# Seven of the 24 modulation chunks of a two-layer diffusion trunk are weighed on the vector engine instead of the tensor engine

## The reference, cut to what matters

```python
mod = jax.nn.silu(cvec) @ w_mod[l] + b_mod[l]            # (1024,) @ (1024, 6144), one row for each of the 2 blocks
sh1, sc1, g1, sh2, sc2, g2 = jnp.split(mod[:, None, :], 6, axis=-1)
h = rms_norm(x, norm_mix[l]) * (1.0 + sc1) + sh1
x = x + g1 * mixer(h)       # l = 0: differential attention and gated DeltaNet; l = 1: gated MLP with a spatial product
h = rms_norm(x, norm_ffn[l]) * (1.0 + sc2) + sh2
x = x + g2 * hier_moe(h)    # 32 experts in 4 groups, the best 2 of one group for each token
```

## Time and profile before

| what | value |
|---|---|
| time, median of 3 runs (lowest to highest) | 803.41 us (802.33 to 806.38) |
| the profiled execution: its own time / its span | 802.09 / 800.3 us |
| PE busy, share of the span | 738.1 us, 92% |
| PE weight loads busy | 490.7 us, 61% |
| DVE busy / ACT busy / POOL busy | 307.1 us (38%) / 163.0 us (20%) / 18.1 us (2%) |
| DMA traffic | 291.49 MB, mean 364 GB/s |
| mean granted PE clock | 0.976 |

### The profile page before, as it was taken

How to read it: one execution, slowest core, us unless ns; L and a number is a source line. 1 busy time by engine, 2 the same in 40 slices (tenths; PEclk the granted TensorE clock), 3 DMA queues, 4 the chain that set the end, 5 groups by cost and what they waited for, 6 DMA issues and landing times.

```text
span 800.3 us, 15774 instructions
## 1 busy us (share of the span) xinstructions
PE 738.1 (92%) x6831; PEld 490.7 (61%) x6831; DVE 307.1 (38%) x680; ACT 163.0 (20%) x319; POOL 18.1 (2%) x29
## 2 busy tenths in 40 slices
PE   3999999998999999999967799999999999995887
PEld 2788467677789745655544244689965655553435
DVE  1144668572512633433440232224353433443024
ACT  3113231233212411111110033031141111111013
POOL 0000001011210000000000000001000000000000
PEclk9999999999999999999998899999999999998798
DMA  9999979496899899999999999999689999999992
GB/s 341 386 372 382 344 267 350 160 327 215 249 373 405 335 422 421 408 421 419 422 420 416 402 386 386 386 406 389 215 314 423 417 399 420 421 421 421 415 399 97
DMA packets 90648, 291.49 MB, mean 364 GB/s; under 512 B 11769, under 2 KB 14927, under 8 KB 73167
## 3 DMA queue, kind: packets, MB, share of 16 engines
q1 hardware_dynamic: 79728, 284.32, 91.0%
q10 hardware_dynamic: 10847, 6.12, 2.7%
HBM read 288.32 MB, written 2.10 MB: 363 GB/s over the span
## 4 chain that ended last, share of the span: by engine, by line
PE 74%; SPq 13%; DMA 7%; ACT 2%; DVE 2%; issue 2%; ACTq 0%; DVEq 0%
PE psum L1346 7%; PE psum L928 7%; PE psum L1430 7%; PE psum L1445 7%; SPq L768 6%; PE psum L1420 6%; PE psum L1480 5%; PE psum L1007 5%; PE psum L881 5%; PE psum L1621 3%; PE psum L1639 3%; PE psum L1491 3%; SPq L786 3%; PE psum L1072 2%; DMA wrt<-in_w_router_expert 2%; DMA ring<-in_w_exp_up 2%
## 5 line engine op out<-in xcount | busy, mean ns | idle before, releaser
L1430 PE MATMUL psum<-ring,hT 128*32 128x512 f32 (+1 forms) x304 | 74.5, 612 | 12.4 <-DMA scratch<-in_w_exp_up 12.4
L1430 PE MATMUL psum<-scratch,hT 128*32 128x512 f32 (+1 forms) x368 | 74.5, 624 | 11.8 <-DMA ring<-in_w_exp_up 11.8
L1420 PE MATMUL psum<-scratch 128*128 128x128 f32 x640 | 75.5, 276 | 0.0
L1420 PEld LDWEIGHTS psum<-scratch 128*128 128x128 f32 x640 | 73.2, 192 | 1.7 <-issue 1.7
L928 PE MATMUL psum<-hT,ring 128*128 128x256 f32 x256 | 57.8, 382 | 1.1 <-DVE hT L2186 0.6
L928 PEld LDWEIGHTS psum<-hT,ring 128*128 128x128 f32 x256 | 47.8, 190 | 9.6 <-DVE hT L2186 2.0
L1491 PEld LDWEIGHTS psum<-const,scratch 128*128 128x128 bf16 x432 | 40.5, 97 | 18.2 <-issue 12.4
L1491 PE MATMUL psum<-const,scratch 128*128 128x256 bf16 x432 | 50.4, 272 | 0.2 <-DVE scratch L2638 0.2
L2003 ACT ACTIVATE scratch<-psum 128x256 f32<-128x256 f32 x20 | 7.7, 384 | 198.1 <-PE psum L1430 124.5
L2631 DVE TENSOR_SCALAR hT<-psum,const 128x512 f32<-128x512 f32 x20 | 15.0, 751 | 85.7 <-PE psum L1480 84.2
L1430 PEld LDWEIGHTS psum<-ring,hT 128*32 128x32 f32 (+1 forms) x304 | 19.7, 117 | 43.3 <-issue 43.3
(11 more groups left out here) (354 smaller groups left out, 991.8 us busy)
## 6 DMA issues: line engine op xcount, KB each, us to landing
ring<-in_w_mod SPq DMA_DIRECT2D x40, 1024.0 KB, 11.7
scratch<-in_w_exp_down SPq DMA_DIRECT2D x32, 1024.0 KB, 17.0
ring<-in_w_exp_down SPq DMA_DIRECT2D x24, 1024.0 KB, 18.1
scratch<-in_w_exp_gate SPq DMA_DIRECT2D x22, 1024.0 KB, 17.5
scratch<-in_w_exp_up SPq DMA_DIRECT2D x22, 1024.0 KB, 19.5
ring<-in_w_exp_gate SPq DMA_DIRECT2D x18, 1024.0 KB, 17.4
ring<-in_w_exp_up SPq DMA_DIRECT2D x18, 1024.0 KB, 20.1
scratch<-in_w_exp_gate SPq DMA_DIRECT2D x24, 512.0 KB, 9.1
```

The lines of the kernel that those rows point to most:

```text
L1420: last = mm(bank[b][:, k * P:(k + 1) * P], hrow[:, t, half * 4 + k, :], Pm[:, t, :], start=(t == 0), stop=(t == 1))
L1430: last = mm(bank[0][i * m:(i + 1) * m, :], xg[:, k, i * m:(i + 1) * m], w[e][:, k, :, :], start=(k == 0), stop=(k == KT - 1))
```

## The change

The matrix product of a chunk is a sum over the 8 rows `k` and over the 128 partitions. For the seven chunks in `SUMMED` the sum over `k` moves to DVE: `weigh_rows` goes over the 8 rows and the 2 token blocks with one instruction of 128 x 512 each, the first two a product with a scalar, the other 14 a fused multiply-add, and leaves the two sums in rows 0 and 1 of the chunk's own slot. PE then only adds over the partitions, with stationary operands [1 0] and [0 1]: 8 products in place of 32. Each `weigh_rows` waits until the whole chunk has landed, and PE waits for the new semaphore `v_acc`. Four further things move: PE uses (0,7) and (0,9) where (0,6) and (0,8) stood, and (0,6) and (0,8) after them; (1,5) follows `in1` 3; in the middle SP loads (1,10) ahead of `in1` 0 and (1,11) ahead of `in1` 1; the turning of group `M_B` is later on all three engines. `v_abx` and `t_u` are folded into other semaphores.

```diff
+SUMMED = [(0, 6), (0, 8), (0, 10), (0, 11), (1, 5), (1, 10), (1, 11)]
...
-        put_mods(0, 6, 7)
+        put_mods(0, 7, 6)
         put("in0", 0)
-        put_mods(0, 8, 9)
+        put_mods(0, 9, 8)
...
+        middle = [index[s] for s in (("mod", 1, 4), ("in1", 2), ("mod", 1, 5), ("in1", 3), ("mod", 1, 10), ("in1", 0), ("mod", 1, 11),
+                                     ("in1", 1), ("out1", 0), ("out1", 1))]
...
+        chosen = [const[:, C_J8 - 1:C_J8 + 1], const[:, C_I32:C_I32 + 2]]
...
@@ mod_chunk, PE
-                if g > M_HI and nth == 0:
+                if g > M_HI:
                     pe.wait_ge(S.v_mod, g)
+                if (l, j) in SUMMED:
+                    pe.wait_ge(S.v_acc, 2 * KT * (SUMMED.index((l, j)) + 1))
+                    for t in range(NB):
+                        for m in range(4):
+                            last = mm(bank[mbank[g]][32 * m:32 * m + NB, at:at + P], chosen[t], w[:, 1 - t, m * P:(m + 1) * P],
+                                      start=(t == 0), stop=(t == NB - 1))
+                    used(last)
+                    return
...
@@ PE, layer 0
             last.then_inc(S.t_ab, 1)
-            mod_chunk(0, 6)
+            mod_chunk(0, 7)
             pe.wait_ge(S.a_sqc, 2)
...
             length_sums()
-            mod_chunk(0, 7)
             length_rows()
+            mod_chunk(0, 6)
...
-            mod_chunk(0, 8)
+            mod_chunk(0, 9)
             pe.wait_ge(S.a_qkv, 1)
...
-            mod_chunk(0, 9)
+            mod_chunk(0, 8)
...
@@ PE, the middle
             for j in range(2):
-                if j == 1:
-                    mod_chunk(1, 5)
                 s = chunk_full(pe, ("in1", 2 + j))
...
-            mod_turn(M_B)
+            mod_chunk(1, 5)
...
@@ DVE
+            def weigh_rows(l, j, k0=0, k1=KT):
+
+                w = slot_kn(chunk_full(dve, ("mod", l, j)))
+                done = 2 * KT * SUMMED.index((l, j))
+                early = part(E0 + 8704, (512,)) if (l, j) in ((0, 6), (0, 8)) else const[:, C_LEV:C_LEV + 512]
+                for k in range(k0, k1):
+                    for t in range(NB):
+                        out = early if t == 0 and k < 2 else w[:, 1 - t, :]
+                        if k == 0:
+                            if t == 1:
+                                dve.wait_ge(S.v_acc, done + 1)
+                            ins = V.tensor_scalar(out, w[:, k, :], condT[:, t, k:k + 1], None, ALU.mult)
+                        else:
+                            dve.wait_ge(S.v_acc, done + (4 if k == 2 else 2 * k - 1 + t))
+                            ins = V.scalar_tensor_tensor(out, w[:, k, :], condT[:, t, k:k + 1], early if t == 0 and k == 2 else out, ALU.mult, ALU.add)
+                        ins.then_inc(S.v_acc, 1)
...
             conv_rows(2)
+            weigh_rows(0, 6)
             dve.wait_ge(S.t_ab, 2)
...
             V.tensor_copy(gcc, bank[6][:, 0:16]).then_inc(S.v_gd, 1)
             dve.wait_ge(S.v_gd, 2)
+            weigh_rows(0, 8, 0, 5)
...
+            weigh_rows(0, 8, 5, KT)
             qkv_rows(1, 5)
...
             later_values(1)
             for t in range(NB):
+                weigh_rows(0, 10, 3 * t, 3 * t + 3)
                 dve.wait_ge(S.a_ors, NB + t + 1)
...
@@ moe(l), DVE
+                if l == 0:
+                    weigh_rows(0, 10, 6, KT)
                 shift_row(l)
                 if l == 1:
                     dve.wait_ge(S.v_mod, M_B + 1)
+                else:
+                    weigh_rows(0, 11, 0, 1)
                 dve.wait_ge(S.t_wo, 2 * l + 1)
                 residual(l, 0, 0, 4)
                 if l == 0:
                     modulation(M_4)
+                    weigh_rows(0, 11, 1, 4)
                 dve.wait_ge(S.used, index[(name, 0)] + 1)
                 residual(l, 1, 0, 4)
+                if l == 0:
+                    weigh_rows(0, 11, 4, KT)
...
             norm(3, 1, 0)
-            modulation(M_B)
+            weigh_rows(1, 5)
+            weigh_rows(1, 10)
...
+            weigh_rows(1, 11)
+            modulation(M_B)
             dve.wait_ge(S.a_lnr, 1)
```

More of the change, by code:

```diff
@@ L280, in __init__ @@
         self.v_ab = sem("v_ab")
-        self.v_abx = sem("v_abx")
+        self.v_acc = sem("v_acc")
         self.v_att = sem("v_att")
@@ L426, in build @@
         flat = hT[:, :, :, :].rearrange("p k t n -> p (k t n)")
-        mrow = [wrt[:, :, :, :].rearrange("p l k n -> p (l k n)")[:, 0:512]] * 5 + [part(2048, (512,)), flat[:, D:D + 512], part(0, (512,)), flat[:, D:D + 512]]
+        mrow = [wrt[:, :, :, :].rearrange("p l k n -> p (l k n)")[:, 0:512]] * 5 + [part(2048, (512,)), flat[:, D:D + 512], const[:, C_LEV + 512:C_LEV + 768], flat[:, D:D + 512]]
         mbank = [7] * 6 + [5, 3, 5]
@@ L585, in build @@
         put("in1", 2)
+        put("in1", 3)
         put_mods(1, 5)
-        for j in (3, 0, 1):
+        for j in range(2):
             put("in1", j)
@@ L594, in build @@
         index = {s: n for n, s in enumerate(stream) if s[0] != "moe"}
+        middle = [index[s] for s in (("mod", 1, 4), ("in1", 2), ("mod", 1, 5), ("in1", 3), ("mod", 1, 10), ("in1", 0), ("mod", 1, 11),
+                                     ("in1", 1), ("out1", 0), ("out1", 1))]
+        loaded = list(range(moe_at[0], moe_at[0] + MOE_SLOTS)) + middle + list(range(moe_at[1], len(stream) + 3))
         loads = ([(("mod", 0, 0), "all"), (("mod", 0, 2), "all"), (("in0", 3), "low"), (("in0", 4), "low"),
@@ L629, in build @@
             place[c], prior[c], held[at] = at, None if at >= RING else last_in[at], c
-        for c in range(moe_at[0] + len(turns), len(stream) + 3):
+        for c in loaded[len(turns):]:
             if c == moe_at[1]:
@@ L651, in build @@
             quarters.update((moe_at[l] + MOE_SLOTS - 2, moe_at[l] + MOE_SLOTS - 1))
-        for c in range(moe_at[0], len(stream)):
+        for c in loaded[:len(stream) - moe_at[0]]:
             count[slot_of(c)] += 64 if c in quarters else 16 if c in singles else 32
@@ L829, in _ @@
             moe_further(0)
-            for c in range(moe_at[0] + MOE_SLOTS, moe_at[1]):
+            for c in middle:
                 load(stream[c], "all")
@@ L1629, in _ @@
                 if j == 1:
-                    pe.wait_ge(S.v_mod, M_B + 1)
+                    mod_turn(M_B)
                     pe.wait_ge(S.ld_router, 16 * 10)
@@ L1637, in _ @@
                     b = 2 * j + m // 2
+                    if b == 3 and m == 2:
+                        pe.wait_ge(S.v_mod, M_B + 1)
                     for k in range(KT):
@@ L1641, in _ @@
                     if m == 1:
-                        last.then_inc(S.t_u, 1)
+                        last.then_inc(S.t_v, 1)
                 used(last)
@@ L1734, in mod_row @@
             def mod_row(g):
-                act.wait_ge(S.used, index[("mod",) + MODS[g][-1]] + 1)
+                act.wait_ge(S.used, max(index[("mod",) + m] for m in MODS[g]) + 1)
                 if g > 0:
@@ L1856, in _ @@
             roots()
-            act.wait_ge(S.v_abx, 1)
+            act.wait_ge(S.v_ab, 2)
             A(t16a, t16a, ACT.Exp).then_inc(S.a_e1, 1)
@@ L2261, in _ @@
             link(V.tensor_tensor(lamq, lamq, lamk, ALU.mult))
-            V.tensor_reduce(lame, lamq.rearrange("p (a n) -> p a n", a=2), AX.X, ALU.add).then_inc(S.v_abx, 1)
+            V.tensor_reduce(lame, lamq.rearrange("p (a n) -> p a n", a=2), AX.X, ALU.add).then_inc(S.v_ab, 1)
             convolve(2)
```

5 lines of the change are left out of this document (2 added, 3 removed).

## The result

| | before | after |
|---|---|---|
| median of the runs | 803.19 us (800.14 to 807.60, 10 runs) | 808.71 us (803.78 to 816.91, 10 runs) |
| ratio of the runs, 95% interval | | 1.0081 [1.0054, 1.0107] |
| profiled execution, own time | 802.09 us, clock 0.976 | 803.78 us, clock 0.972 |

The change makes the kernel 6.5 us slower (0.0081 x 802), where I forecast 0.4 us faster: 808.7 lies outside the range of 799.5 to 806.5. The profiled execution of after is the fastest of its ten; two later profiles of the same kernel took 814.03 and 814.44 us.

What follows compares the result with a forecast made beforehand. PE fills three quarters of the span; only time won outside the DMA-full expert stretches counts. +0.5 us before 280 us and -2.9 in the middle gave -2.4; 2.0 clock loss left -0.4: 803.4 to 803.0 us, range 799.5 to 806.5.

Steps and rivals of the forecast that it cites:

- Together -2.4 us, if PE's clock stays: Sum over all seven chunks: +0.5 us before 280 us and -2.9 us in the middle, without any clock loss.
- (0,6): wait and clock: Layer 0, 70 to 93 us: late DVE moves PE's token product by 3.1 us; slower clock costs 2.0 more.
- the other six: Gains: (0,8), (1,5), (1,10) 1.39 us each, (0,10) 1.1, (0,11) and (1,11) 0.1 each.
- is where the change pays: At (0,6) DVE's idle 9.61 us is shorter than the chunk's 10.3, so the token product moves by 3.1 us.
- The clock's term: Two PE idle times around 80 to 86.4 us lower the clock to 0.50, costing 0.8 to 3.0 us; 2.0 taken.
- the middle's 2.9: Between the layers (1,5) and (1,10) gain 1.4 us each and (1,11) 0.1, hidden in DVE's idle times.
- The case by which POOL's scaling delays the shift: At (0,10), POOL's 1.61 us scaling falls under DVE's last rounds; if all is added, the shift is 0.7 us late.
- The 0.3 us put there: At (0,10), the cost taken from 0 to 0.7 us of shift delay, leaving a net gain of 1.1.
- A: Rival: same mechanism but no slow clock stretch at (0,6), 801.0 us; chance 0.22.
- B: Rival: DVE's sums bound layer 0, each step taking 0.745 us, delaying (0,6) and (0,10): 806.0 us; chance 0.12.
- D: Rival: DMA, by in1's later loads or the full stretches, swallows the middle's gain: 805.9 us; chance 0.07.
- C: Rival: (0,11) and (1,11) give 1.39 us each in full and the clock holds: 798.4 us; chance 0.12.

Runs made afterwards that it cites:

- before_p138: Kernel before with 138 more PE instructions of long fulfilled waits, so its jump stands at 241 as in the changed kernel: 807.07 us, ratio 1.0063.
- after_p118: Changed kernel with 118 more PE instructions of long fulfilled waits, so its jump stands at 103 as in the kernel before: 802.85 us, ratio 1.0019.
- only06: Kernel before with chunk (0,6) alone weighed on DVE and put behind the row lengths, (0,7) ahead of it: 812.75 us, ratio 1.0134.
- only06_p95: only06 with 95 more PE instructions of fulfilled waits, moving its jump from 8 to 103: 807.06 us, ratio 1.0072 to the kernel before.
- hot: Changed kernel with five float32 128x256 products in each of PE's two idle times at (0,6): 805.87 us, ratio 1.0049 to the kernel before.
- hot_p78: Changed kernel with float32 filler in PE's two idle times and 78 more fulfilled-wait instructions, jump at 103: 801.91 us, ratio 0.9996 to the kernel before.
- no06: Changed kernel with (0,6) given back to PE and both chunks in their old places, other six still summed: 796.67 us, ratio 0.9937 to before.
- mid: Kernel before with only the three middle chunks (1,5), (1,10) and (1,11) weighed on DVE: 800.28 us, ratio 0.9978.
- after_c: Changed kernel unaltered, run once for a third profile: 814.44 us.
- early06: Changed kernel with the load of (0,6) issued two transfers earlier: 809.93 us, ratio 1.0083 to the kernel before.
- order06: Kernel before with only the places of (0,6) and (0,7) exchanged, both full PE products: 806.47 us, ratio 1.0052.
- warm: Changed kernel with 8 and 7 bf16 products of zeros on 32 rows in PE's two idle times: 810.94 us, ratio 1.0095 to the kernel before.

## Why the prediction was wrong

**The failed step** is the sum, in that it had only terms of work, waits and the clock behind them: "Together -2.4 us, if PE's clock stays", and -0.4 with the clock. It held no term for PE's code. The prediction counts the records that PE sheds and never asks where that moves the rest of its program. Shortened by 374 instructions ahead of the jump, PE's program has the jump at 241 in place of 103 behind a multiple of 256, and there PE waits 2.4 to 5.3 us for the block that it jumps into; the clock falls behind that. Moving the jump is worth 5.0 us [2.6, 7.5] by before_p138 alone, and about the same from after to after_p118 and from only06 to only06_p95 (0.0062 each) and from hot to hot_p78 (0.0053), each known to some 3 us.

| term | forecast | measured |
|---|---|---|
| (0,6): wait and clock | +3.1 and +2.0 | +5.8 [4.4, 7.2], only06_p95 |
| the other six | -5.5 | -5.0 [-7.0, -3.2], no06 |
| the jump (padding alone) | none | +5.0 [2.6, 7.5], before_p138 |
| sum | -0.4 | +5.8; +6.5 measured on the whole |

**(0,6).** Right in each step: the load, DVE's end, the two idle times of PE, 3.1 us of wait (3.28 in hot). The clock's term was a little small: 2.6 us in the trace, 2.6 from after to hot. That (0,6) "is where the change pays" for the others was right, and it pays more than they bring: left out, the change gains.

**The other six.** Right as a sum. Of the middle's 2.9 us mid gives 1.8 [0.3, 3.2], which can't tell them apart. The case by which POOL's scaling delays the shift did not come: POOL did take 1.47 us longer, which agrees in kind with what the prediction quotes of the Trainium skill, "SBUF — State Buffer", section "SBUF: two separate sides". But it was mainly POOL that lost time, while DVE's four products beside it took 3.10 us against 2.73 by their pace of 0.663, and the shift was in time. The 0.3 us put there cost PE nothing.

**The rivals.** A (the clock holds) is hot: 3.9 us slower than before, not 2.4 faster. With the jump moved as well, hot_p78 stands at -0.3 us [-2.1, +1.4]; the 2 us between it and A, at -2.4, are just outside this interval, and its two slow stretches could hold them. That is argued, not shown. B, at 806.0, and D, at 805.9, came nearest to the measured time, and that is luck: B's reason is false. DVE's last eleven steps of (0,6) were 0.663 us apart, below its point of decision (0.68; by its own terms 0.673), and PE waited for no shift. C and D did not happen: the six chunks gained what they should and no more (no06), and the middle's gain was not swallowed (mid).

**The chances.** I gave slower 0.14. All cases but one were built from the same list of causes; the range of 7 us held the costs that I knew and no room for one that I did not. The profile before had the hint: issue of 0.98 and 1.38 us between like products, on an engine that had nothing to wait for.

```profile
181.62 0.91 PE L1072 MATMUL psum<-scratch 64*64 64x64 f32 x23 [0.98 <-issue]
...
187.95 1.15 PE L1072 MATMUL psum<-scratch 64*64 64x64 f32 x32 [1.38 <-issue]
```

There, too, a packet of code had landed some 1.5 us earlier, at 180.0 and 186.5 us.

**Open.** Why the wait at the jump is 2.4 us in some executions and 5.3 in others. In the second case the packet starts about 2.5 to 2.7 us after PE's last product, in place of within 0.2; the DMA engines are full in both (share 1.05), and what orders it was not tried. And whether the same jump in layer 1 costs regularly: PE is idle there for 2.1 to 2.7 us in three of seven profiles with its position between 252 and 26 (after_c and before_p138, named issue, and early06, named ACT), in none of eleven with 36 to 144. The padding takes this jump into that range in before_p138 and out of it in after_p118, so their 5.0 us may hold a part of it. In only06, only06_p95, hot and hot_p78 it stands outside, and there the 0.0062 and 0.0053 are layer 0's alone.

## What to carry to other kernels

An edit that changes how many instructions an engine runs ahead of a jump moves the jump against the blocks in which its program is loaded; compare the engine's idle time by "issue" before and after, beside the waits with a releaser. Before the terms of a sum are blamed, take out the change but keep its length of code: a kernel with only padding (before_p138) showed 5 us that no step of the work explains. And of several like edits, one that ends up late can eat the gain of all: here six are worth -5.0 us and the seventh +5.8.

## What the runs showed of the hardware

- PE waits for its own code. It resumed some 1.5 us after a packet of 16 KB had landed, in all nine profiles that have the idle time at the end of layer 0, whether it was 2.4 or 5.3 us long.
- The clock fell to 0.50 within a single uncovered idle time of 2.50 us (order06, early06), and all the same where bf16 products of zeros on 32 rows filled the idle times (warm, PE busy for 3.47 of the 3.70 us before). Five float32 products of 128x256 in each gap held it at 1.00 (hot).
- A fulfilled wait is not free: 512 of them held PE for 25.46 us, two to an instruction, so about 0.1 us an instruction (an estimate that puts all of the idle time on them).
- Four products of POOL beside DVE's products with two SBUF inputs took 3.08 us in place of 1.61.
